# Where the split weights lie in SBUF: weight slots 32, 96, 160 and 224 bytes behind the tiles of h

## The reference, cut to what matters

```python
h    = modulate(rms_norm(x, g), shift, scale)           # 256 tokens x 1024
q    = h @ w_query                                      # 8 heads x 2 x 128
top  = top_k over the sums of two top-16 key scores     # 16 experts a head
w    = softmax(top scores)
y    = sum over chosen experts e of  w_e * gelu(h . u_e) * v_e
out  = rms_norm(x + gate * y, final_g)
```

## Time and profile before

| | us |
|---|---|
| median of 3 runs | 1348.43 |
| lowest and highest | 1346.44, 1349.39 |
| the profiled execution | 1346.72 |
| its span, first to last instruction | 1345.4 |
| TensorE busy (matmul) | 1280.8 |
| VectorE busy | 1063.8 |
| ScalarE busy | 596.4 |
| GpSimd busy | 252.7 |

### The profile page before, as it was taken

How to read it: one execution, slowest core, us unless ns; L and a number is a source line. 1 busy time by engine, 2 the same in 40 slices (tenths; PEclk the granted TensorE clock), 3 DMA queues, 4 the chain that set the end, 5 groups by cost and what they waited for, 6 DMA issues and landing times.

```text
span 1345.4 us, 21959 instructions
## 1 busy us (share of the span) xinstructions
PE 1280.8 (95%) x8283; PEld 1114.5 (83%) x8283; DVE 1063.8 (79%) x2318; ACT 596.4 (44%) x1105; POOL 252.7 (19%) x180
## 2 busy tenths in 40 slices
PE   5988999988999899999999999999999999999997
PEld 5577855685697569999999999999988888888886
DVE  5587896787777688999997888888977777777776
ACT  1434683536344535455544444444343333343342
POOL 0363000450000006789950000000000000000001
PEclk9999999999999899999999999999999999999999
DMA  9877631867577245554444444444455555555552
GB/s 356 290 231 271 235 137 60 300 210 264 206 278 273 104 168 178 173 185 158 171 143 156 142 147 152 142 156 141 157 204 191 199 189 196 194 191 196 191 192 106
DMA packets 92382, 256.82 MB, mean 191 GB/s; under 512 B 9472, under 2 KB 16896, under 8 KB 91904
## 3 DMA queue, kind: packets, MB, share of 16 engines
q1 hardware_dynamic: 59728, 195.91, 42.0%
q10 hardware_dynamic: 32560, 59.66, 12.4%
HBM read 254.47 MB, written 1.06 MB: 190 GB/s over the span
## 4 chain that ended last, share of the span: by engine, by line
PE 62%; DVE 13%; POOL 8%; issue 7%; DMA 5%; ACT 3%; SPq 1%; POOLq 0%; ACTq 0%; DVEq 0%
PE bank L1734 25%; PE bank L1727 19%; PE bank L691 5%; PE bank L2006 4%; PE bank L1121 3%; POOL v_lo L1766 2%; POOL u_lo L1766 2%; DVE arena L432 2%; DVE arena L968 2%; PE bank L799 2%; DMA arena<-in_w_in 2%; POOL head_ms L822 2%; DMA arena<-in_nsa_w_in 1%; DVE u_lo L683 1%; ACT arena L976 1%
## 5 line engine op out<-in xcount | busy, mean ns | idle before, releaser
L1727 PE MATMUL bank<-h_hi,u_hi 128*128 128x256 f32 x632 | 182.8, 289 | 3.9 <-POOL u_lo L1766 2.8
L1727 PE MATMUL bank<-h_hi,u_lo 128*128 128x256 f32 x632 | 178.7, 283 | 0.0
L1727 PE MATMUL bank<-h_lo,u_hi 128*128 128x256 f32 x632 | 178.7, 283 | 0.0
L1727 PEld LDWEIGHTS bank<-h_hi,u_hi 128*128 128x128 f32 x632 | 121.0, 191 | 4.7 <-POOL u_lo L1766 1.9
L2163 POOL TENSOR_SCALAR raw<-raw 128x1024 f32<-128x1024 f32 x1 | 3.4, 3356 | 631.7 <-DMA raw<-in_final_g 631.7
L1727 PEld LDWEIGHTS bank<-h_lo,u_hi 128*128 128x128 f32 x632 | 121.1, 192 | 0.0
L1727 PEld LDWEIGHTS bank<-h_hi,u_lo 128*128 128x128 f32 x632 | 120.9, 191 | 0.0
L2102 ACT ACTIVATE u_hi<-raw 128x1024 fp32r<-128x1024 f32 x64 | 67.9, 1061 | 104.4 <-PE bank L1734 104.4
L1727 PE MATMUL bank<-h_hi,v_hi 128*128 128x256 f32 x392 | 112.8, 288 | 0.8 <-POOL v_lo L1766 0.8
L2102 ACT ACTIVATE v_hi<-raw 128x1024 fp32r<-128x1024 f32 x64 | 67.9, 1061 | 101.1 <-PE bank L1734 101.1
L1727 PE MATMUL bank<-h_hi,v_lo 128*128 128x256 f32 x392 | 110.8, 283 | 0.0
(11 more groups left out here) (275 smaller groups left out, 3486.5 us busy)
## 6 DMA issues: line engine op xcount, KB each, us to landing
raw<-in_u SPq DMA_DIRECT2D x128, 512.0 KB, 3.5
raw<-in_v SPq DMA_DIRECT2D x128, 512.0 KB, 4.3
arena<-in_ada_t SPq DMA_DIRECT2D x80, 512.0 KB, 5.2
arena<-in_ada_w SPq DMA_DIRECT2D x12, 512.0 KB, 12.2
raw<-in_nsa_w_in ACTq DMA_DIRECT2D x3, 2048.0 KB, 12.0
arena<-in_moba_w_in ACTq DMA_DIRECT2D x3, 2048.0 KB, 16.5
arena<-in_w_in ACTq DMA_DIRECT2D x3, 2048.0 KB, 10.3
arena<-in_w_query ACTq DMA_DIRECT2D x3, 2048.0 KB, 10.7
```

The costliest lines, as they stand in the source:

```text
L1727: last = pe.matmul(zbank[k].t[:, 0:S], u[:, c, :], h[:, c, :], start=n == 0, stop=n == 3 * DC - 1)
```

## The change

The tiles are allotted in another order, with small unused tiles (`apart_...`, 8 words = 32 bytes or 16 words = 64 bytes a partition) between them. No instruction is added, removed or moved, on any engine; only the addresses change.

```diff
-    split = {}
-    for name in ("u", "v"):
-        split[name] = [[sb(f"{name}_{part}{k}", [P, D], F32R) for k in range(2)] for part in ("hi", "lo")]
-    quad = [(split[n][0][k][:], split[n][1][k][:]) for n in ("u", "v") for k in range(2)]
     h_hi, h_lo = sb("h_hi", [P, DC, S], F32R), sb("h_lo", [P, DC, S], F32R)
     raw_all = sb("raw", [P, 4, D])
-    a_hi, a_lo = ([sb(f"a_{part}{k}", [P, S], F32R) for k in range(2)] for part in ("hi", "lo"))
+    split, sides = {name: [[None, None], [None, None]] for name in ("u", "v")}, [[None, None], [None, None]]
+    for name, k, apart in (("u", 0, 8), ("a", 1, 8), ("u", 1, 8), ("v", 0, 16), ("v", 1, 16), ("a", 0, 8)):
+        sb(f"apart_{name}{k}", [P, apart])
+        for part, parts in zip(("hi", "lo"), sides if name == "a" else split[name]):
+            parts[k] = sb(f"{name}_{part}{k}", [P, S if name == "a" else D], F32R)
+    a_hi, a_lo = sides
+    quad = [(split[n][0][k][:], split[n][1][k][:]) for n in ("u", "v") for k in range(2)]
```

## The result

| | before | after |
|---|---|---|
| median, us | 1348.79 (4 runs) | 1359.09 (4 runs) |
| lowest and highest, us | 1346.44, 1349.39 | 1356.84, 1360.66 |
| profiled execution and its span, us | 1346.72, 1345.4 | 1356.84, 1355.5 |

The ratio is 1.0081 with a 95% interval from 1.0061 to 1.0100: the change makes the kernel 10.3 us slower, where 37 us less were forecast.

A forecast was written before the change was run, and what follows sets the result against it. TensorE's matmul step was taken to bound stages B and C, three engines together stage A. Gains of 16.0 + 15.8 + 2 + 3.5 = 37.3 us took the profiled 1346.7 to 1309.4, median 1311; range 1301 to 1352.

The forecast's parts named there:

- the slower case: Rival: 32 bytes bring the two operand streams together, 4.2 ns lost per product, 21 us in all, 1370 us; chance 0.20.
- a step that differs from slot to slot: Sign of a wrong prediction: the distance would then matter beyond its being an odd multiple of 32 bytes.
- TensorE's step: Matmul-to-matmul step: skewed operand starts remove excess, 8.3 ns gained per 256-column product, 10.3 ns per 512-column product.
- stage C: Third expert stage, 1536 products of 512 columns: 10.3 ns gained on each, 15.8 us.
- stage B: Second expert stage, 2112 products of 256 columns: 17.5 us gained, less 1.5 us for late groups, 16.0 us.
- layers and stage A: Layers' products gain 3.5 us; first expert stage gains 2 us, the rest of TensorE's 8.0 us going into waits for GpSimd.
- No change: Rival: the excess is a fixed handover between weight load and fp32r matmul, blind to addresses; 1348 us, chance 0.20.
- Half: Rival: the skew removes only some encounters, or those of one of the two shapes; 1330 us, chance 0.15.
- GpSimd and VectorE take all: Rival for all of stage A and part of B: 6 us of B's gain lost to VectorE; 1317 us, no separate chance.

The follow-up runs named there:

- the chains alone: Kernels with only fp32r matmul chains, whole computation left out, one chain per distance between tile starts; at distance 0, 120.0 ns (256 columns) and 227.5 ns (512).

## Why the prediction was wrong

**What held.** The reading of the profile held: stages B and C hang on TensorE's step alone, the step holds 13 ns that are not arithmetic, and that time depends on addresses (those of the two operands, with no other engine at work). Plain float32 products kept their step (L2008: 0.89 us for 8 records, 111 ns, in both). Stage A gave nothing back, because VectorE and GpSimd end it. The settled step of L1734 over 227 ns was named as the mark of the slower case. The sign "a step that differs from slot to slot" came as well, in z: 118.2, 118.0, 119.8 and 116.8 ns. That the other engines take nothing from shifted tiles also held: in stages B and C VectorE's lo takes 1219 and 1225 ns a record against 1219 and 1226 before, ScalarE's hi 1063 and 1062 ns against 1063 and 1061. The 231 ns after a restart lie near the 233 ns of a bad distance; no run shows that the two have one cause.

**The step that failed** is "TensorE's step", in the part on the change: "Both readers start at the same place modulo 256 bytes", from which it was taken that equal starts are the worst place and that a skew takes the excess away. For the 512-column shape equal starts are the best of all distances tried, 226.7 ns against 227.8 to 240.0. The terms against what they became:

| term | forecast, us | measured, us | shown by |
|---|---|---|---|
| stage C | -15.8 | +9.3 | 1500 steps of 233.1 against 226.9 ns; a alone skewed gives it, distance 0 takes it back |
| stage B | -16.0 | -2.1 | chain of work, first gate group to last z |
| layers and stage A | -5.5 | +2.9 | start of the first gate group |
| sum | -37.3 | +10.1 | spans |

**Stage B** had the right sign and an eighth of the size. Not one of the four distances with h is a good one: 118.3, 118.6, 120.0 and 117.8 ns in the chains alone, against the 111.7 that the sum used. The floor was taken from another kind of product (plain float32); for this shape no chain went under 113.3.

**Layers and stage A.** Nothing of the 3.5 us forecast for the layers shows: z starts at 557.8 us, where it started at 557.6, and this start differs by more than that from profile to profile, as said above. The loss lies between the first z product and the first gate group: 137.8 us against 135.0. In the kernel after, the chain of work of this stretch runs through VectorE. The kernel with a alone skewed, whose z step is the old one, has 135.0 us there as well; the eight whole kernels with a shorter z step have 135.9 to 137.8. One instruction of VectorE makes 2.2 of the 2.8 us. It starts at 657.25 us in both kernels, and a subtraction of GpSimd starts just behind it before, and just ahead of it after (its row holds two subtractions, one behind the other). Before, VectorE and GpSimd:

```profile
657.25 2.29 DVE L1927 TENSOR_TENSOR arena<-arena,iota_k 128x2048 f32<-128x2048 f32 x1
657.38 8.85 POOL L1766 TENSOR_TENSOR u_lo<-raw,u_hi 128x1024 fp32r<-128x1024 f32 x2 [1.05 <-ACT u_hi L1764]
```

After:

```profile
657.22 6.80 POOL L1768 TENSOR_TENSOR u_lo<-raw,u_hi 128x1024 fp32r<-128x1024 f32 x2 [0.92 <-ACT u_hi L1766]
657.25 4.51 DVE L1929 TENSOR_TENSOR arena<-arena,iota_k 128x2048 f32<-128x2048 f32 x1
```

This line has four such instructions in each of the ten profiles of whole kernels. Without exception they take 2.3 us where the next subtraction of GpSimd starts behind them, and 4.4 to 4.5 us where one had started before them. The third of the four is short in the two with the old z step and long in the eight with a shorter one. So with the faster z GpSimd's subtraction starts 0.16 us earlier and thus ahead of VectorE's instruction, and the selection, whose end the gates wait for, became longer. The forecast counted on 4.8 us of idle time of VectorE and had no term for this. The other 0.6 us stay open.

**The rivals.** "Slower" was the case that came, at its mark; its price was 4.2 ns for each product of both shapes, and it is 6.2 ns in C and less than nothing in B, so that 1370 was too high. "No change" as the fixed handover is refuted by the chains. "Half" supposed that one geometry gains and one does not; the geometries did part, but one of them lost. "GpSimd and VectorE take all" came true in stage A; in B some 2.1 of the 2.4 us that the steps give back (118.55 against 119.73 ns, some 2000 of them) arrived.

**What stays open.** What the distance acts on. It has a period of 256 bytes in all pairs of chains but one, a grain of a few bytes, two states for one and the same pair of addresses, and no simple relation to the length of the weight load. Which part of TensorE holds such a state, and what sets it at an interruption, no run shows.

## What to carry to other kernels

The start addresses of the two tiles of an fp32r matmul relative to each other, modulo 256 bytes, are worth up to 6% of its step, and the sign depends on the shape. Measure the step of each shape for the distances at hand with a chain of some 50 matmuls before moving tiles, and more than once behind different work, since one distance can have two settled steps: here distance 0 was best for 512 columns and 64 for 256 columns, and setting only those (h at 192) gave 0.9951 and 0.9966 of the time before, while the skew of everything cost 0.8%. An excess over arithmetic in the trace shows neither that it can be gained nor which way: the present place can be the best one, as distance 0 was for 512 columns, with 13.4 ns of excess.

## What the runs showed of the hardware that was not expected

- Distance 0 gives 226.7 ns for 512 columns, 4 bytes more give 237.3 and 68 bytes give 239.4; 252 bytes (4 less than 0) give 228.8.
- The settled step of one chain is exact over dozens of matmuls (120.0, 113.3, 226.7, 233.3 ns), yet distance 64 settles at 113.3 or at 117.8 ns for 256 columns, for the same addresses, in two kernels and within one. The state holds through hundreds of products and changes only at an interruption; with h at 192 every gate group changed it.
- Two kinds of instruction of different engines got in each other's way by order alone: a VectorE tensor_tensor of 128x2048 with both inputs in SBUF took 2.3 us when GpSimd's subtraction started 0.13 us or more behind it, and 4.4 to 4.5 us when it had started 0.03 to 0.3 us before.
- The Trainium skill, page "SBUF - State Buffer" (Who interferes with whom), says that TensorE waits on no one and has two read ports of its own. No effect of other engines on the step was seen here, which agrees. But the distance between its own two operands moved the step from 113.3 to 120.0 ns and from 226.7 to 240.0 ns, with no other engine at work.
- Fewer weight columns can lengthen or shorten the step of a 512-column product: at distance 0 it is 231.7 ns with 32 columns against 226.7 with 128, at distance 32 it is 226.7 ns against 232.9.
